# Making a mixture-of-experts layer's shared down products in one early expert pass and parking three of them in SBUF

## The reference

```python
def moe_tokens(h, p):                      # h (T, D)
    scores = sigmoid(h @ p['w_router'])
    ...                                    # group-limited top 8 of 64 experts
    gate = ...                             # (T, 64), eight non-zero entries a row
    hg = einsum('td,edf->tef', h, p['w1']) # w1, w3: 64 x 1024 x 256
    hu = einsum('td,edf->tef', h, p['w3'])
    act = silu(hg) * hu * gate[:, :, None]
    routed = einsum('tef,efd->td', act, p['w2'])                   # w2: 64 x 256 x 1024
    shared = (silu(h @ p['ws1']) * (h @ p['ws3'])) @ p['ws2']      # ws2: 256 x 1024
    return routed + shared
...
x = x + gate2 * rmsnorm(moe(h), g_post2)
```

## Time and profile before

| | us |
|---|---|
| median of 3 runs | 1251.86 |
| lowest, highest run | 1251.62, 1254.39 |
| span of the profiled execution | 1254.6 |
| TensorE busy in it | 1175.3 (94%) |
| VectorE, ScalarE, GpSimd busy | 560.5, 327.8, 524.8 |

### The profile page before, as it was taken

One profiled execution on the slowest core, in us unless ns is written; L12 is line 12 of the kernel. 1 busy time (PEld: TensorE's weight loads), 2 busy tenths in 40 slices (PEclk: granted clock), 3 DMA queues, 4 the chain that ended last, 5 costly groups with the idle time before them and its releaser, 6 DMA issues.

```text
span 1254.6 us, 25608 instructions
## 1 busy us (share of the span) xinstructions
PE 1175.3 (94%) x8959; PEld 844.7 (67%) x8960; DVE 560.5 (45%) x912; ACT 327.8 (26%) x620; POOL 524.8 (42%) x527
## 2 busy tenths in 40 slices
PE   4899999999999899969899999998999998999897
PEld 3699999999999899958654555544455554554442
DVE  4285667658668868137632322221112221222134
ACT  3523322322333532335211121111111211111122
POOL 2144444444457344400644455442344445354420
PEclk9799999999999899989998999998999999999899
DMA  9954344425421133348779899999999999999977
GB/s 309 324 164 152 103 131 150 150 84 163 148 74 48 54 105 96 118 168 327 276 275 389 337 391 410 409 409 412 410 409 411 409 405 401 407 406 401 369 280 275
DMA packets 157224, 337.44 MB, mean 269 GB/s; under 512 B 14807, under 2 KB 99363, under 8 KB 139753
## 3 DMA queue, kind: packets, MB, share of 16 engines
q1 hardware_dynamic: 137496, 296.57, 63.6%
q0 software_dynamic: 16656, 34.14, 7.2%
q10 hardware_dynamic: 3025, 6.07, 1.4%
HBM read 322.21 MB, written 33.30 MB: 283 GB/s over the span
## 4 chain that ended last, share of the span: by engine, by line
PE 65%; SPq 14%; DMA 7%; issue 6%; DVE 6%; POOL 1%; ACT 1%; DVEq 0%; POOLq 0%; ACTq 0%
PE ps L1746 19%; PE ps L1509 10%; PE ps L1510 9%; PE ps L1511 9%; PE ps L1757 9%; SPq L356 8%; DMA w<-in_w_dram 4%; SPq L361 4%; DMA ring<-in_w_ada_dram 2%; PE ps L1522 1%; PE ps L1752 1%; PE ps L1849 1%; PE ps L1451 1%; PE ps L1816 1%; SPq L388 1%
## 5 line engine op out<-in xcount | busy, mean ns | idle before, releaser
L1746 PE MATMUL ps<-w,xe 128*64 x3136 | 371.3, 391 | 32.0 <-DMA w<-in_w_dram 22.4
L1746 PEld LDWEIGHTS ps<-w,xe 128*64 128x64 f32 x3136 | 226.8, 141 | 173.8 <-issue 73.8
L534 POOL TENSOR_TENSOR wsplit<-ring,wsplit 128x1024 fp32r<-128x1024 f32 x80 | 194.6, 2432 | 282.5 <-ACT wsplit L687 252.4
L1509 PE MATMUL ps<-h_s_hi,wsplit 128*128 128x260 f32 x960 | 272.2, 283 | 0.0
L1511 PE MATMUL ps<-h_s_hi,wsplit 128*128 128x260 f32 x960 | 270.7, 282 | 0.0
L1510 PE MATMUL ps<-h_lo_m_hi,wsplit 128*128 128x260 f32 x832 | 234.8, 282 | 0.0
L1371 DVE TENSOR_TENSOR rs<-sg,ps 128x128 f32<-128x128 f32 x98 | 28.2, 288 | 386.7 <-ACT sg L985 386.7
L1757 PE MATMUL ps<-w,eactT 128*64 (+1 forms) x784 | 187.3, 598 | 0.0
L1509 PEld LDWEIGHTS ps<-h_s_hi,wsplit 128*128 128x128 f32 x960 | 180.6, 188 | 6.7 <-issue 5.9
L1511 PEld LDWEIGHTS ps<-h_s_hi,wsplit 128*128 128x128 f32 x960 | 180.8, 188 | 0.0
L687 ACT ACTIVATE wsplit<-ring 128x1024 fp32r<-128x1024 f32 x80 | 84.9, 1061 | 296.6 <-PE ps L1511 286.3
(11 more groups left out here) (333 smaller groups left out, 1331.8 us busy)
## 6 DMA issues: line engine op xcount, KB each, us to landing
w<-in_w_dram SPq DMA_DIRECT2D x192, 1024.0 KB, 19.2
ring<-in_w_in_dram SPq DMA_DIRECT2D x56, 512.0 KB, 3.9
ring<-in_w_ada_dram SPq DMA_DIRECT2D x8, 2048.0 KB, 8.8
ring<-in_w_ada_dram SPq DMA_DIRECT2D x8, 1024.0 KB, 24.9
ring<-y_rows SPq DMA_DIRECT2D x4, 2048.0 KB, 16.2
ring<-in_w_out_a_dram SPq DMA_DIRECT2D x8, 512.0 KB, 4.1
ring<-in_w_out_b_dram SPq DMA_DIRECT2D x8, 512.0 KB, 4.1
ring<-in_w_o_dram SPq DMA_DIRECT2D x8, 512.0 KB, 4.0
```

The costliest lines, as they stand in the source:

```text
L534: pool.tensor_tensor(wsplit[:, b, 1], raw[raw_slot], wsplit[:, b, 0], ALU.subtract).then_inc(S["w_lo"], 1)
L1509: mm(ps[:, bank + h, 0:HT], wsplit[:, b, 0, k, :], hi[:, k, p:q], start=(k == 0), stop=False)
L1746: ins = mm(ps[a * STRIP:(a + 1) * STRIP, 2 + f, 0:2 * P], xe[:, k, a * STRIP:(a + 1) * STRIP], w[a][:, k, :, f * P:(f + 1) * P], start=(k ...
```

## The change

All five shared down products are made at the head of the sixteenth pass (`SHARED_AT = 15`), in banks 6, 7, 0 and 1. ScalarE copies the sums of tiles 2, 3 and 4 to SBUF (`park`, into `xflat`); those of tiles 1 and 0 stay in banks 0 and 6. In the tail a product with the identity (`unpark`, two products with 512 columns) puts a parked sum back in PSUM, where `shared_down` stood. `ws2` is loaded from ScalarE's queue at the head of the eleventh pass (`WS2_AT = TT`, pairs of passes). Since `xflat` is taken, `split` becomes four separate blocks of 512 KB, loaded by four transfers instead of two. In the tail the early half of tile 3 moves ahead of the last half of tile 2, and SP waits for the five products before it loads the first y rows.

```diff
-        split = [(xflat[:, 0:3 * D], 3), (slot_part(5, YF + D, D), 1)]
+        split = [(hflat[:, 0:D], 1), (xflat[:, 3 * D:4 * D], 1), (sflat[:, 2 * T:2 * T + D], 1), (slot_part(5, YF + D, D), 1)]
+        parked = [xflat[:, 0:D], xflat[:, D:2 * D], xflat[0:NS, 2 * D:3 * D]]
+        WS2_AT, SHARED_AT = TT, 15
...
-            with sp.Fori(1, 4) as g:
-                for u in range(DEEP):
-                    refill(g * DEEP + u, g * DEEP + (u - DEEP), u)
-            sp.wait_ge(S["late_chain"], LA * TT)
-            for k in range(FT):
-                sp.dma_start(ws2_in[k], ws2[0, k * P:(k + 1) * P, :]).then_inc(w_late, 16)
-            with sp.Fori(4, E // DEEP) as g:
+            with sp.Fori(1, E // DEEP) as g:
...
             rows_there(0)
+            sp.wait_ge(S["sh_mm"], 2 * FT + TT)
...
+            def park(n):
+                act.wait_ge(S["sh_mm"], 2 * FT + n + 1)
+                bank = (6, 0, 6)[n]
+                src = ps[0:NS if n == 2 else P, bank:bank + 2, :]
+                act.activation(parked[n], src.rearrange("p b n -> p (b n)"), ACT.Copy).then_inc(S["sh_ev"], 1)
...
             with act.Fori(0, pairs) as it:
                 for u in range(2):
+                    if u == 0:
+                        with act.If(it == WS2_AT):
+                            act.wait_ge(S["late_chain"], LA * TT)
+                            for k in range(FT):
+                                act.dma_start(ws2_in[k], ws2[0, k * P:(k + 1) * P, :]).then_inc(w_late, 16)
+                    else:
+                        with act.If(it == SHARED_AT // 2):
+                            for n in range(3):
+                                park(n)
                     one_pass(it * 2 + u, u)
...
+            def shared_down(i, f):
+                rows = P if i < TT - 1 else LAST
+                for h in range(2):
+                    for k in range(FT):
+                        ins = mm(ps[0:rows, f + h, :], scr[:, 2 + k, i * P:i * P + rows], ws2_in[k][:, h * 512:(h + 1) * 512],
+                                 start=(k == 0), stop=(k == FT - 1 and i > 1))
+                ins.then_inc(S["sh_mm"], 1)
+            def unpark(n):
+                bank, rows = (2, 4, 6)[n], (P, P, NS)[n]
+                for h in range(2):
+                    mm(ps[0:rows, bank + h, :], ident[0:rows, 0:rows], parked[n][:, h * 512:(h + 1) * 512], start=True, stop=False)
+            def shared_downs():
+                pe.wait_ge(w_late, 16 * C + 64)
+                shared_down(2, 6)
+                shared_down(3, 0)
+                pe.wait_ge(S["sh_ev"], 2 * FT + 1)
+                shared_down(TT - 1, 6)
+                pe.wait_ge(S["sh_ev"], 2 * FT + 2)
+                shared_down(1, 0)
+                pe.wait_ge(S["sh_ev"], 2 * FT + 3)
+                shared_down(0, 6)
...
+                        with pe.If(p == SHARED_AT):
+                            shared_downs()
                         pe.wait_ge(S["xe_dve"], p * 2 + 1)
...
-            pe.wait_ge(w_late, 16 * C + 64)
-            shared_down(0)
-            shared_down(1)
...
             pe.wait_ge(S["gm_dve"], 2)
-            shared_down(2)
-            pe.wait_ge(y_first_in, 16 * TT)
+            pe.wait_ge(y_first_in, 16 * (3 + len(split)))
             mark(gated_rows(0, 1, y_first), "early_pe")
             gated_rows(1, 1, y_first)
             pe.wait_ge(S["xe_dve"], passes * 2 + 2)
             last_sums(0)
+            unpark(0)
             pe.wait_ge(S["ex_yd"], passes + 2)
-            shared_down(3)
+            unpark(1)
             last_sums(1)
             gated_rows(2, 1, y_first)
+            gated_rows(3, 1, y_first)
             last_sums(2)
-            gated_rows(3, 1, y_first)
             pe.wait_ge(S["yacc"], 1)
-            shared_down(TT - 1)
+            unpark(2)
             last_sums(TT - 2)
```

More of the change, by code:

```diff
@@ L154, in whole @@
             return [(t, 4)]
-        split = [(xflat[:, 0:3 * D], 3), (slot_part(5, YF + D, D), 1)]
-        y_first = [split] + [whole(t) for t in (slot_part(5, 0, YF), slot_part(0, 0, YF), slot_part(1, 0, YF))]
-        y_last = [whole(t) for t in (slot_part(2, 0, YF), slot_part(3, 0, YF), slot_part(4, 0, YF))] + [split]
         ws2_in = [hflat[:, 0:D], xflat[:, 3 * D:4 * D]]
@@ L208, in build_program @@
         xgs = [sflat[:, 0:D], conv[:, 0:D]]
+        split = [(hflat[:, 0:D], 1), (xflat[:, 3 * D:4 * D], 1), (sflat[:, 2 * T:2 * T + D], 1), (slot_part(5, YF + D, D), 1)]
+        y_first = [split] + [whole(t) for t in (slot_part(5, 0, YF), slot_part(0, 0, YF), slot_part(1, 0, YF))]
+        y_last = [whole(t) for t in (slot_part(2, 0, YF), slot_part(3, 0, YF), slot_part(4, 0, YF))] + [split]
+        parked = [xflat[:, 0:D], xflat[:, D:2 * D], xflat[0:NS, 2 * D:3 * D]]
         esil, eact = sg[:, 0:256], rs[:, 0:256]
@@ L1808, in expert @@
                         down_product(down, 1, 1).then_inc(S["ex_y"], 1)
[L1810 to L1817, removed]
             with pe.Fori(0, 5) as g:
@@ L1844, in gated_rows @@
                 i, f = order[n], bank_of[n]
+                blocks = [part[:, a * D:(a + 1) * D] for part, n_ in src[i] for a in range(n_)]
                 for c in range(2):
                     for b in range(4):
-                        part, n = src[i][0] if b < src[i][0][1] else src[i][1]
-                        at = b % n * D + c * 512
-                        ins = mm(ps[32 * b:32 * b + 32, f + c, :], gmat[:, b, i, h, :], part[:, at:at + 512],
+                        ins = mm(ps[32 * b:32 * b + 32, f + c, :], gmat[:, b, i, h, :], blocks[b][:, c * 512:(c + 1) * 512],
                                  start=False, stop=(h == 0))
```

## The result

The changed kernel took 1253.70 us in the median of 12 runs (1252.91 to 1256.20), the kernel before, beside it on the same chip, 1251.45 (12 runs, 1250.00 to 1255.86). The ratio is 1.0022, 95% interval 1.0012 to 1.0032: 2.8 us slower, 1.5 to 4.0. The forecast was -0.1 us. 1253.70 lies in the range, and within the 0.3% that the prediction names as no change, but the sum is off by more than the measurement leaves open: the change makes the kernel slower.

What follows compares the result with a forecast made beforehand. The expert-weight stream sets the pace from 740 to 1160 us, TensorE close beside it. Sum 3.0 - 4.8 + 0.9 + 0.8 = -0.1 us, giving 1251.8 from the median 1251.86; range 1247 to 1258.

Steps and rivals of the forecast that it cites:

- The stop at 674: TensorE's stop at the first loop turn's end goes; TensorE 6.0 us earlier, weights 4.8: -4.8 us, ends -4.8 and 0.
- Hole: 0.4: First gap in the weight stream from later asks: landing at 830.0 against 829.6 unbroken, 0.4 us; a second is 3.4.
- The hole: Sixteenth pass delays SP's asks by 17.8 us, so the weight stream has gaps: +3.0 us, ends 0 and +5.
- The sign set for a larger hole: A DMA share below 0.9 at 826 to 842 us would show that the hole is larger than forecast.
- The stops of new code: New jumps in the last four passes, where nothing hides them, add one stop: +0.9 us, ends 0 and +1.
- The tail: After the last pass, TensorE waits for the last y rows, then runs at half clock: +0.8 us, ends -1.7 and +0.8.
- TensorE's 5.1 us: Tail work saved as three identity products replace three shared ones; rival that it pays in full: 1245.9 us, chance 0.13.
- the rival of +28: The loop's longer code no longer stays loaded, a stop at every turn's end: +28 us, 1280, chance 0.11.
- The load from ScalarE's queue: Shared weights loaded from ScalarE's queue five passes ahead of use, same bytes: 0; its two issues uncovered would cost 0.8 us.
- the parking copies: ScalarE's three copies of 1.02 us each lie under TensorE's 17.8 us: taken as 0, 3 us if uncovered.
- SP's wait: SP waits for the five products ahead of the first y rows; claimed to be over long before, no cost added.

Runs made afterwards that it cites:

- four_pieces: The kernel before with the y rows of tile 3 loaded in four pieces instead of two, all products where they were: +2.0 us over before.
- before_again: The kernel before, unchanged, run for a second profile: +0.7 us (-0.4 to +1.9), no difference.
- jump_first: The kernel before plus never-taken code of 80 products in the first expert loop's six bodies alone: -1.9 us against before.
- jump_first_again: Repeat of the kernel before with never-taken code of 80 products in the first loop's six bodies alone: -3.4 us against before.
- late_first: The changed kernel with the five shared products in the twentieth pass and their code in the first loop alone: 1250.08 us, -0.8 against before.
- first_only: The changed kernel, products still in the sixteenth pass, their code in the first loop's six bodies alone: 1253.53 us, +3.1 over before.
- stall_only: The kernel before plus five unused products of the same size in the sixteenth pass, code in all 16 bodies: +3.1 us over before.
- pieces_first: The kernel before with never-taken code in the first loop and tile 3's y rows in four pieces: -2.8 us against before.
- jump_only: The kernel before plus never-taken code of the same 80 products in all 16 bodies, no shared product moved: -0.1 us against before.
- after_again: The changed kernel, unchanged, run for a second profile: +3.9 us (2.6 to 5.1) over before.
- code_once: The changed kernel with the shared products' code only in the one body that runs the sixteenth pass: +4.6 us over before (five runs).
- three_two_again: Repeat of the changed kernel with three shared products in the sixteenth pass and two between the expert loops: +4.4 us over before.

## Why the prediction was wrong

The table is worked out from the packets in the traces. It follows the queue that moves the expert weights: the time (us) at which 140, 130 and 30 MiB of all that it moves until the end were left. The stop is TensorE's near 672. "First" is the start of the first pass (us), which differs from profile to profile.

```
                  first    stop    140 MiB  130 MiB  (took)   30 MiB
before            623.6    2.98     817.4    847.6    30.2    1143.2
four_pieces       624.1    1.78     814.6    844.5    29.9    1140.0
before_again      624.1    0.41     812.6    842.8    30.2    1137.7
jump_first        624.0    none     811.6    841.8    30.2    1137.9
jump_first_again  621.9    none     809.4    839.7    30.3    1136.2
late_first        622.6    none     809.9    840.1    30.2    1136.6
after             623.1    none     809.8    846.6    36.8    1142.6
first_only        622.6    none     809.0    846.0    37.0    1142.3
stall_only        622.6    none     809.6    845.2    35.6    1143.0
```

*The stop at 674: the step that failed.* The forecast took it as gone, and it is gone in every profile of the change. But "Then TensorE is 6.0 us earlier, and the weights by what the DMA idled until 740 ... 4.8" took its price from one execution. Part of the differences between the first five rows is there before the stop: the passes begin up to 2.2 us apart. Counted from the first pass, the weights (140 MiB) are 6.3 us behind jump_first_again's with the stop of 2.98 us, 3.0 with 1.78, some 1 with 0.41, and 0.2 in jump_first, without one. So the 4.8 was not too much for the profile that it was read from; but that is the far end of what varies, and the sum took it off the median. In the runs the stop's absence is worth 1.9 and 3.4 us (jump_first twice) and 2.8 (pieces_first), 2.7 in the mean. The term is -2.7 where the sum had -4.8: 2.1 us of the 2.4 to 2.9 that are missing.

*The hole: right in its cause, and too small.* Ten MiB took 30 us without the stall and 36 to 37 with it. The asks moved and landed as worked out; what failed is "Hole: 0.4", which let the stream run full until the last landing. The sign set for a larger hole, a DMA share below 0.9 at 826 to 842, did not come (.91), because the working left out that the passes stand 6.7 us earlier: the hole lies at 812 to 821, with a share of .55. In the time of the runs the hole is worth 3.4 (first_only against late_first) or 3.2 (stall_only against jump_only), up to 5 if stall_only is set against jump_first; the sum had 3.0. That this comes so near is luck, since twice as much of the stream was lost. What arrives is the lag of the weights for the pass near 1170: they land 3.8 us later in first_only than in late_first (1169.89 against 1166.09), and 3.5 later in stall_only than in jump_only (1168.49 against 1165.03). Why not all of the 6.3 us arrives is not traced: the lag of first_only behind late_first is 7.1 us at 60 MiB left and 5.7 at 30 MiB. Why late_first lies 1.0 us behind jump_first is open: its tail, in its profile, is 0.9 us the shorter.

*The stops of new code* came where they were expected, behind 1160, and also at 926.86, for which the sum had nothing. At 1173.25 it was 1.2 us over the 0.46 from landing to start that before's second profile shows. By the runs it is 0.8 (after_again +3.9, first_only +3.1) or, with the +2.8 of the result, -0.3: not distinguishable from nothing behind the hole, and 1.8 to 3.3 us without a hole (jump_only against jump_first twice). The sum had +0.9.

*The tail* did in the mean what was forecast. From the end of the last pass's products to the end of the span, the eight profiles with before's products take 34.2 to 34.5 us; the seven with the changed tail take 33.3, 34.1, 34.6, 34.6, 34.9, 36.7 and 36.7, 35.0 in the mean: +0.8, as in the sum. The change's own two are 34.1 and 34.6, and the spread is new: the tail now ends on a load, which took 8.2 us in late_first (tail 33.3), 8.8 in the change (34.1) and 11.2 in code_once (36.7); in three_two_again (36.7) it took 9.1, so it isn't all of it. TensorE's 5.1 us bought nothing, since the last rows start when they land, 21.1 to 23.8 us after the last pass, with three identity products or none.

*The rest.* The loop stayed loaded: q8 is not listed from 680 to 880 us in the changed kernel either, so the rival of +28 falls. The load from ScalarE's queue, the parking copies and SP's wait were costed at nothing, and stall_only, which has none of them, loses as much. The prediction's list of waits leaves out those at 846.14 (1.56 us), 897.93 (1.28) and 1063.79 (5.40); no term of the sum hangs on them. Put together, -2.7 + 3.4 + 0.8 + 0.8 = +2.3, against the 2.25 between the medians and the 2.8 of the ratio. Each of these terms is uncertain by a microsecond or more, so that they meet the total is no proof of each.

## What to carry to other kernels

Work that is to be hidden behind a stream of loads belongs where its engine already waits for that stream: the 17.7 us cost some 3.4 us more in the sixteenth pass, with nothing for TensorE to wait for, than in the twentieth, where they left the stream full. A stop that the profile shows is the stop of one execution; before its removal is booked as a gain, take a second profile and see where the profiled execution lies among the timed ones. When a tail waits for a load, taking work from the engine that waits buys nothing.

## What was not expected of the hardware

The DMA engines did not stay full until the last transfer had landed: with asks 22.5 us apart the rate fell from 418 GB/s at 811 us to 53 at 818, the last landing being at 819.7.

The same place in the same code stopped TensorE for 0.41, 1.78 and 2.98 us in three executions (before_again, four_pieces and before, whose passes have the same code). Never-taken code of 80 records in six loop bodies removed the stop, and with it 1.9 and 3.4 us; with the same code in the other ten bodies too the time was that of before, and at the first of the four bodies behind the loops a wait of 5.17 us named "issue" stood, where 3.38 us for weights stand without it.
